# Attention of a hybrid decoder layer at three places of the order of work in place of seven

## The reference

```
h = rmsnorm(x, g_mix);  proj = h @ w_in            # columns: q, k, v (512 each), u (2 x 512), two gates (1024 each)
o = moba_attention(q, k, v)                         # 8 heads of 64; one block of 256, so plain causal attention
branch_a = o @ w_attn_up
z = u_a * sigmoid(u_g);  z = causal depthwise conv(z), 31 taps;  z = silu(layernorm(z))
branch_c = z @ w_conv_pw + b_conv_pw
x = x + (sigmoid(gate_a) * branch_a + sigmoid(gate_c) * branch_c) @ w_out
h = rmsnorm(x, g_ffn);  x = x + relu(h @ w_ff1)^2 @ w_ff2
return rmsnorm(x, g_final)
```

## Time and profile before

| | |
|---|---|
| median of 3 runs | 351.67 us |
| span of the profiled execution | 350.3 us |
| TensorE (PE) busy | 344.2 us, 98% |
| VectorE (DVE) busy | 251.5 us, 72% |
| ScalarE (ACT) busy | 192.1 us, 55% |
| chain of work that ended last | TensorE 98% of the span |

### The profile page before, as it was taken

One profiled execution on the slowest core, in us unless ns is written; L12 is line 12 of the kernel. 1 busy time (PEld: TensorE's weight loads), 2 busy tenths in 40 slices (PEclk: granted clock), 3 DMA queues, 4 the chain that ended last, 5 costly groups with the idle time before them and its releaser, 6 DMA issues.

```text
span 350.3 us, 4670 instructions
## 1 busy us (share of the span) xinstructions
PE 344.2 (98%) x1766; PEld 289.5 (83%) x1766; DVE 251.5 (72%) x313; ACT 192.1 (55%) x236; POOL 3.5 (1%) x13
## 2 busy tenths in 40 slices
PE   8999999999999999999999999999999999999994
PEld 5889988787778888888888888888888888889884
DVE  2969999899999889965666946639466394563813
ACT  4985644698796358434674535515355163551534
POOL 1000000000000000000000000000000000000000
PEclk9999999999999999999999999999999999999998
DMA  8999455534353365783647472944729537260003
GB/s 278 349 387 377 155 206 156 206 122 153 121 198 130 120 239 156 265 254 110 198 157 227 152 252 90 299 180 128 248 102 301 178 121 243 115 239 0 0 0 120
DMA packets 34429, 64.23 MB, mean 183 GB/s; under 512 B 1360, under 2 KB 6000, under 8 KB 34416
## 3 DMA queue, kind: packets, MB, share of 16 engines
q1 hardware_dynamic: 34056, 63.56, 54.0%
q10 hardware_dynamic: 360, 0.49, 0.4%
HBM read 63.00 MB, written 1.05 MB: 183 GB/s over the span
## 4 chain that ended last, share of the span: by engine, by line
PE 98%; DVE 0%; issue 0%; DVEq 0%; ACT 0%
PE ps L971 20%; PE ps L972 19%; PE ps L973 19%; PE ps L1230 17%; PE ps L1238 9%; PE ps L958 4%; PE ps L1018 2%; PE ps L1122 1%; PE ps L1121 1%; PE ps L1123 1%; PE ps L1029 1%; PE ps L1072 1%; PE ps L1097 1%; PE ps L998 1%; PE ps L1191 0%; PE ps L1282 0%
## 5 line engine op out<-in xcount | busy, mean ns | idle before, releaser
L971 PE MATMUL ps<-w_hi,a_lo 128*128 128x512 f32 x256 | 100.9, 394 | 0.0
L972 PE MATMUL ps<-w_hi,a_hi 128*128 128x512 f32 x256 | 99.8, 390 | 0.0
L973 PE MATMUL ps<-w_lo,a_hi 128*128 128x512 f32 x256 | 99.7, 390 | 0.0
L899 DVE TENSOR_TENSOR w_lo<-raw,w_hi 128x2048 fp32r<-128x2048 f32 x28 | 63.5, 2287 | 6.2 <-ACT w_hi L623 6.2
L405 ACT CAST w_hi<-raw 128x2048 fp32r<-128x2048 f32 (+1 forms) x30 | 53.7, 1799 | 19.9 <-PE ps L973 19.7
L1230 PE MATMUL ps<-b_both,w_hi 128*128 128x512 f32 x256 | 61.3, 390 | 0.0
L674 DVE TENSOR_TENSOR w_lo<-raw,w_hi 128x2048 fp32r<-128x2048 f32 x26 | 59.3, 2285 | 1.7 <-ACT w_hi L405 1.7
L623 ACT CAST w_hi<-raw 128x2048 fp32r<-128x2048 f32 x28 | 52.8, 1914 | 7.5 <-PE ps L973 7.5
L971 PEld LDWEIGHTS ps<-w_hi,a_lo 128*128 128x128 f32 x256 | 48.1, 188 | 10.1 <-issue 0.5
L973 PEld LDWEIGHTS ps<-w_lo,a_hi 128*128 128x128 f32 x256 | 48.0, 188 | 10.2
L972 PEld LDWEIGHTS ps<-w_hi,a_hi 128*128 128x128 f32 x256 | 48.1, 188 | 9.4
(11 more groups left out here) (138 smaller groups left out, 302.5 us busy)
## 6 DMA issues: line engine op xcount, KB each, us to landing
raw<-in_w_ff_dram SPq DMA_DIRECT2D x32, 1024.0 KB, 5.4
raw<-in_w_in_dram SPq DMA_DIRECT2D x14, 1024.0 KB, 5.9
raw<-in_w_out_dram SPq DMA_DIRECT2D x4, 1024.0 KB, 5.3
raw<-in_w_in_dram SPq DMA_DIRECT2D x14, 256.0 KB, 5.7
raw<-in_w_attn_up_dram SPq DMA_DIRECT2D x2, 1024.0 KB, 5.2
raw<-in_w_conv_pw_dram SPq DMA_DIRECT2D x2, 1024.0 KB, 5.1
res<-in_x_dram SPq DMA_DIRECT2D x2, 512.0 KB, 3.9
raw<-in_w_in_dram SPq DMA_DIRECT2D x4, 128.0 KB, 4.1
```

Source lines behind the costliest of these rows:

```text
L899: nc.vector.tensor_tensor(w_lo[:, slot], raw[:, slot], w_hi[:, slot].bitcast(F32), ALU.subtract).then_inc(lo_made, 1)
L971: nc.tensor.matmul(dst, lo[:, tok], w_hi[:, slot, k], start=start, stop=False, skip_group_check=seeded)
L972: nc.tensor.matmul(dst, hi[:, tok], w_hi[:, slot, k], start=False, stop=False, skip_group_check=seeded)
L973: return nc.tensor.matmul(dst, hi[:, tok], w_lo[:, slot, k], start=False, stop=stop, skip_group_check=seeded)
```

## The change

Scores, transposes and values are each done for two pairs at a time. The second pair of a group gets buffers of its own: banks `(4, 5)` and `(6, 7)` by `pair_banks(p)` for scores and later for the transposed blocks, and two parts of `nat` that are free then for probabilities and their transposed copy. Scores of pairs 0 and 1 stand behind unit 9, of 2 and 3 behind unit 12. Transposes of a group of two stand inside units 12 and 15, after the first tile of tokens, and its values behind the same unit. Outputs of pairs 0 and 1 go to bank 2, emptied by one copy of both, and block 5 is taken from that bank before (now in `take`'s usual place); unit 14, which writes bank 2, waits for that copy. The transposes of the convolution move from behind unit 16 into unit 17.

On ScalarE the converts around the scores move: the one of iteration 10 (unit 13) to iteration 9, ahead of the exponentials, the one of iteration 13 (unit 16) likewise to 12; at 12 and 15 the convert stands behind the copies of the probabilities. On VectorE the maxima of two pairs stand at the top of iterations 9 and 12, both inverses with three convolution steps between them behind the split; the convolution steps are dealt out anew; the layer norm goes with `S_LN` from iteration 16 to 17.

```diff
-S_ATT = 9
+S_SCORES = {9: (0, 1), 12: (2, 3)}
+S_VALUES = (12, 15)
+S_O_OUT = 14
+CONV_BETWEEN = 3
-S_OLO = S_ATT + 6
-S_GATE = 14
-S_LN = 16
+S_OLO = 15
+S_GATE = 16
+S_LN = 17
-CONV_AT = {..., 8: 6, 9: 5, 10: 8, 11: 11, 12: 12, 13: 11, 14: 10, 15: 5}
+CONV_AT = {..., 8: 6, 9: 6, 10: 6, 11: 6, 12: 15, 13: 12, 14: 11, 15: 6}
...
+        probs_of = (probs[:], nat[:, 0, 0:768])
+        probs_t_of = (probs_t[:], nat[:, 1, 0:768])
+        def pair_banks(p):
+            return (TB, SB0)[p % 2]
+        def o_pair(p):
+            if p < 2:
+                return ps[:, 2, p * T:p * T + T]
+            return ps[:, pair_banks(p) + 1, T:2 * T]
...
 # ScalarE, iteration n
-                if n and n + AHEAD < U_LOOP + AHEAD_LOOP and n not in GLU_AT:
+                if n and n + AHEAD < U_LOOP + AHEAD_LOOP and n not in GLU_AT and n not in S_VALUES and n - 1 not in S_SCORES:
                     high(n + AHEAD)
+                if n in S_VALUES:
+                    group = S_VALUES.index(n)
+                    probs_out(2 * group)
+                    probs_out(2 * group + 1)
+                    high(n + AHEAD)
+                    o_out(group)
+                if n in S_SCORES:
+                    high(n + AHEAD + 1)
+                    for p in S_SCORES[n]:
+                        exps(p)
+                    for p in S_SCORES[n]:
+                        normalise(p)
...
 # VectorE, iteration n (row_max, then the layer norm at S_LN, then low(n + 3), then:)
+                if n in S_SCORES:
+                    first, second = S_SCORES[n]
+                    inverse(first)
+                    conv_products(n, slice(0, CONV_BETWEEN))
+                    inverse(second)
                 if n != S_OLO:
-                    conv_products(n)
+                    conv_products(n, slice(CONV_BETWEEN if n in S_SCORES else 0, None))
...
 # TensorE, unit n
+                if n == S_O_OUT:
+                    pe.wait_ge(ot_made, 1)
                     unit(n, ...,
                          (lambda: glu_transposed(GLU_AT[n])) if n in GLU_AT else
+                         (lambda: pairs_transposed(S_VALUES.index(n))) if n in S_VALUES else
+                         conv_transposed if n == S_LN else None)
+                if n == S_VALUES[0]:
+                    pe.wait_ge(evac, GA)
+                if n in S_VALUES:
+                    group = S_VALUES.index(n)
+                    values(2 * group)
+                    values(2 * group + 1).then_inc(pv_done, 1)
+                if n in S_SCORES:
+                    for p in S_SCORES[n]:
+                        scores(p)
```

More of the change, by code:

```diff
@@ L60 @@
 CONV += [(tap, c) for tap in range(10, TAPS) for c in range(4)]
-CONV_AT = {2: 6, 3: 12, 4: 9, 5: 9, 6: 9, 7: 7, 8: 6, 9: 5, 10: 8, 11: 11, 12: 12, 13: 11, 14: 10, 15: 5}
+CONV_AT = {2: 6, 3: 12, 4: 9, 5: 9, 6: 9, 7: 7, 8: 6, 9: 6, 10: 6, 11: 6, 12: 15, 13: 12, 14: 11, 15: 6}
 assert len(CONV) == sum(CONV_AT.values()) == (TAPS - 1) * 4
@@ L195, in tile_chunks, with o_group @@
             return ps[:, bank + t, :].rearrange("p (c t) -> p c t", c=4)
-        def o_pair():
-            return ps[:, TB + 1, T:2 * T]
+        def pair_banks(p):
[4 more added lines that the diff above has]
+            return ps[:, pair_banks(p) + 1, T:2 * T]
+        def o_group(group):
+            if group == 0:
+                return ps[:, 2].rearrange("p (c t) -> p c t", c=2)
+            return ps[:, TB + 1:SB0 + 2:2, T:2 * T]
         def chunks(bank):
@@ L475, in exps @@
                 act.wait_ge(nbias_made, p + 1)
+                bank, rows = pair_banks(p), probs_of[p % 2]
                 for h in range(2):
-                    nc.scalar.activation(probs[:, 256 * h:256 * h + 256], ps[:, SB0 + h, 0:256], ACT.Exp,
+                    nc.scalar.activation(rows[:, 256 * h:256 * h + 256], ps[:, bank + h, 0:256], ACT.Exp,
                                          bias=nbias[:, p, h:h + 1], scale=q_scale[:, 1:2], accum_out=psums[:, p, h:h + 1])
                 for h in range(2):
-                    last = nc.scalar.activation(probs[:, 512 + 128 * h:640 + 128 * h], ps[:, SB0 + h, 256:384],
+                    last = nc.scalar.activation(rows[:, 512 + 128 * h:640 + 128 * h], ps[:, bank + h, 256:384],
                                                 ACT.Exp, bias=nbias[:, p, 2 + h:3 + h], scale=q_scale[:, 0:1],
@@ L489, in normalise, with o_out @@
                 for h in range(2):
-                    part = probs[:, 256 * h:256 * h + 256]
+                    part = probs_of[p % 2][:, 256 * h:256 * h + 256]
                     nc.scalar.activation(part, part, ACT.Copy, scale=rinv[:, p, h:h + 1])
                 for h in range(2):
-                    part = probs[:, 512 + 128 * h:640 + 128 * h]
+                    part = probs_of[p % 2][:, 512 + 128 * h:640 + 128 * h]
                     last = nc.scalar.activation(part, part, ACT.Copy, scale=rinv[:, p, 2 + h:3 + h])
                 last.then_inc(norm_made, 1)
-            def o_out(p):
-                act.wait_ge(pv_done, p + 1)
-                nc.scalar.copy(o_t[:, p], o_pair()).then_inc(ot_made, 1)
+            def o_out(group):
+                act.wait_ge(pv_done, group + 1)
+                nc.scalar.copy(o_t[:, 2 * group:2 * group + 2], o_group(group)).then_inc(ot_made, 1)
             def probs_out(p):
                 act.wait_ge(p_tr, p + 1)
-                if p:
-                    act.wait_ge(pv_done, p)
-                nc.scalar.copy(probs_t[:], ps[:, TB:TB + 2, :].rearrange("p b n -> p (b n)")[:, 0:768]).then_inc(pt_made, 1)
+                if p > 1:
+                    act.wait_ge(pv_done, 1)
+                bank = pair_banks(p)
+                nc.scalar.copy(probs_t_of[p % 2], ps[:, bank:bank + 2, :].rearrange("p b n -> p (b n)")[:, 0:768]).then_inc(pt_made, 1)
             def set_bias(col):
@@ L546, in _ @@
                     queries_out()
-                elif n < U_ATTN and n % 2 == 1 and 0 < n // 2 < GA:
+                elif n < U_ATTN and n % 2 == 1 and 0 < n // 2 <= GA:
                     take(n // 2)
[L549 to L557, removed]
+                if n in S_VALUES:
[10 more added lines that the diff above has]
+                        normalise(p)
                 if n < U_ATTN and n % 2 == 1 and n // 2 > GA:
@@ L564, in _ @@
                 if n == S_OLO:
-                    act.wait_ge(ot_made, PAIRS)
+                    act.wait_ge(ot_made, 2)
                     nc.scalar.copy(b_hi[:, 0:CC], o_t[:]).then_inc(o_hi, 1)
@@ L719, in _, with conv_products @@
             low_pair(3, 1, lo_made)
-            def conv_products(step):
-                for m in conv_share(step):
+            def conv_products(step, part=slice(None)):
+                for m in conv_share(step)[part]:
                     tap, c = CONV[m]
@@ L736, in row_max @@
                 dve.wait_ge(mask_made, 1)
-                diagonals = ps[:, SB0:SB0 + 2, P:3 * P]
+                bank = pair_banks(p)
+                diagonals = ps[:, bank:bank + 2, P:3 * P]
                 nc.vector.tensor_tensor(diagonals, diagonals, mask[:].rearrange("p (h s) k -> p h (s k)", h=1).to_broadcast([P, 2, 2 * P]),
@@ L740, in row_max @@
                 dve.wait_ge(masked, p + 1)
-                nc.vector.tensor_reduce(smax[:, p, 0:2], ps[:, SB0:SB0 + 2, 0:256], AX.X,
+                nc.vector.tensor_reduce(smax[:, p, 0:2], ps[:, bank:bank + 2, 0:256], AX.X,
                                         ALU.max).then_inc(max_made, 1)
-                nc.vector.tensor_reduce(smax[:, p, 2:4], ps[:, SB0:SB0 + 2, 256:384], AX.X,
+                nc.vector.tensor_reduce(smax[:, p, 2:4], ps[:, bank:bank + 2, 256:384], AX.X,
                                         ALU.max).then_inc(max_made, 1)
@@ L775, in _ @@
                                                 ALU.mult).then_inc(q_scaled, 1)
-                if n == S_ATT:
+                if n in S_SCORES:
                     dve.wait_ge(q_scaled, 3)
-                if S_ATT <= n < S_ATT + PAIRS:
-                    row_max(n - S_ATT)
+                    for p in S_SCORES[n]:
+                        row_max(p)
                 if n == S_LN:
@@ L864, in _ @@
                     low(n + AHEAD)
-                if S_ATT <= n < S_ATT + PAIRS:
-                    inverse(n - S_ATT)
+                if n in S_SCORES:
[3 more added lines that the diff above has]
+                    inverse(second)
                 if n != S_OLO:
-                    conv_products(n)
+                    conv_products(n, slice(CONV_BETWEEN if n in S_SCORES else 0, None))
                 if n == S_OLO:
@@ L1067, in scores @@
             def scores(p):
+                if p > 1:
+                    pe.wait_ge(pt_made, p - 1)
                 for s, at, keys in ((1, 0, 256), (0, 256, 128)):
@@ L1071, in scores @@
                         rows = slice(HD * h, HD * h + HD)
```

(24 more changed lines are left out.)

6 lines of the change are left out of this document (removed).

## The result

The changed kernel takes 355.21 us (median of 4 runs, 354.84 to 355.96) against 351.53 of the kernel before on the same chip: ratio 1.0104, 95% interval 1.0092 to 1.0116, 3.7 us slower. Forecast were 353.4 us and a range of 352.0 to 356.4: the right side and inside the range, but half of the loss was missing from the forecast.

A forecast was written before the change was run, and what follows sets the result against it. TensorE's own work was taken to bound the kernel. Fewer mode changes (-1.44 us) and a new wait for the normalised rows (+3.2) gave +1.8, added to the median of 351.67: 353.4 us, range 352.0 to 356.4.

The forecast's parts named there:

- The gain of 1.44 us: TensorE, attention between units 9 and 15: 7 changes of the array's mode instead of 15, 8 x 0.18 us saved.
- Joins of one kind: TensorE, groups of one kind side by side: pay nothing between them; full changes at all four joins would take 0.72 us.
- a change of mode: TensorE, switching between full, score and value products: 0.18 us each.
- No cost on ScalarE: Moved converts and later exponentials on ScalarE stay covered by TensorE's units, so they cost nothing.
- The idle time at the third mask: VectorE at the second place reaches the mask at 85.1, scores allow it at 87.8: 2.7 us idle.
- the second inverse: VectorE at the first place waits for the second pair's exponentials: 0.5 us idle.
- The wait itself: TensorE in unit 18 wants the normalised rows at 122.3, VectorE has them at 125.5: 3.2 us.
- Main sum: Whole kernel: gain of 1.44 us against a wait of 3.2 us, +1.8 us.
- rival (a): The wait in unit 18 lowers the granted clock, adding 2.9 us: 356.3 us; chance 0.18.
- The main case: Whole kernel: gain and wait without a fall of the clock, 353.4 us, bounded at 352.4 to 354.2; chance 0.68.
- the engine worked at the lower level of 1.2 GHz: TensorE at the kernel's start: 16 transposes took 3.2 us, 0.2 each against 0.11, read as the lower clock.
- I see no second wait behind: TensorE after the normalised rows in unit 18: no further wait, and nothing that wins the time back.

The follow-up runs named there:

- e10: Changed kernel with nine convolution steps moved from iteration 12 to 11, one from 9 to 8, and a fourth step between the inverses: 350.14 us.
- e2: Changed kernel with seven convolution steps moved from iteration 12 to 11, layer norm still behind the split: 350.82 us.
- e1: Changed kernel with VectorE's layer norm ahead of the split for unit 19 again: 353.32 us.
- e5: Kernel before with only VectorE's layer norm one iteration later, behind the split for unit 19: 351.75 us.
- e9: Changed kernel with seven convolution steps moved from iteration 12 to 11, one from 9 to 8, and a fourth between the inverses: 350.75 us.
- e4: Changed kernel with 12 products of zeros on TensorE ahead of its wait for the normalised rows: 353.65 us.
- e7: Changed kernel with four convolution steps moved from iteration 12 to 11: 351.70 us.

## Why the prediction was right, and where it was not

- **The gain of 1.44 us** was right: -1.43 in D of e10, where no wait is left, and -1.43 in medians (350.14 against 351.57). Joins of one kind cost nothing (the second pair of scores 0.65 against 0.64), a change of mode 0.175, as the mean of two, against 0.18.
- **No cost on ScalarE**: right; behind the start of the kernel no wait of TensorE in any trace is for the probabilities or a convert. Exponentials of the first pair started 4.5 us after the first scores, forecast was 4.6.
- **The idle time at the third mask**: 2.82 us, forecast 2.7; at the second inverse 0.27, forecast 0.5. It is one of three parts of the wait: without it the wait is 0.2 (e2), without the split ahead of the layer norm 0.7 (e1), and the late layer norm alone, without the idle time and the earlier TensorE, makes none (e5). e9 adds that filling idle time is not enough: what counts is how much of VectorE's work stands behind the third mask. The wait itself, counted as the time beyond a full stream, is 124.66 - 121.34 - 0.23 = 3.1 us, forecast 3.2.
- **Main sum**: +1.8 us for a full clock, and e4 gives 1.7 in D and 1.8 in medians (353.65 against 351.86).
- **What failed is the weight of rival (a)**, "Chance 0.18", and its argument "Against it: it is fully busy right up to that wait and again after it". That is no protection: the clock fell all the same, in the trace after and, by their times and clocks (0.988 to 0.993 over the span, with 0.997 in the profile before), in all four runs. The likeliest case should have been main sum plus rival: 351.53 + 1.8 + 2.9 would be 356.2. The price of 2.9 us, from slow work that the forecast put at about 5.9 us without a sum for it, was met in the profiled run (6.0 us of slow work, 2.9 lost in C), which was also the slowest (355.96 us, clock 0.988); in the median of 355.21 it is about 1.9. The main case alone, bounded at 352.4 to 354.2, missed the measured time; the range of 352.0 to 356.4 held only because it took in a rival that I thought unlikely, and that is luck in part. Of the Trainium skill, TensorE: Matmul & The Clock Gate, section HAM oscillation, I had written that by its rule alone 356.3 would be the forecast. That left out the section's condition on the length of a gap, which the wait falls somewhat short of, as forecast (3.2 us) and as measured (2.9). That an idle stretch halves the clock and the work behind it starts slow is what this trace shows (0.50 over 124 to 130.6); that 2.9 us was enough goes beyond the section, and the measurement decides.
- That at the start "the engine worked at the lower level of 1.2 GHz" rests on the pace of the transposes alone (0.2 us against 0.11); the granted clock of the profile reads 1.00 there.
- "I see no second wait behind" held for the changed kernel, but for a reason that I had not seen: e1 shows that VectorE was nearly as late for unit 20, where the forecast had no margin worked out. In the changed kernel the first wait hid this, and it didn't take the slow stretch: e4 has the same delay at a full clock and no wait at unit 20 either.

## What to carry to other kernels

Count the changes of the array's mode (rows by columns of the products), not the places: each costs 0.18 us here, and transposes of full size, at 0.11 us each, paid no change wherever they stood in the stream. When work is grouped on the engine that bounds the time, look at the other engines' programs for an instruction that now waits for the group with independent work queued behind it; that work has to go ahead of it, and it helps only if it crosses that point. And price a wait of the array twice: here 1.4 us of wait cost 1.6 (D of e7 against e10), while 2.9 us of it cost 2.9 more through the clock in the profiled run and 1.9 more in the medians. Where the wait couldn't be removed, products of zeros in it gave that part back (e4).

## What the runs showed that was not expected

The clock fell in the middle of a span in which TensorE was otherwise never idle, behind a wait of 2.9 us (for 6.8 us, until 130.7) and, in four of six runs by their clocks, behind one of 2.2 (for 3.4 us in the trace), not behind 1.4, nor behind 0.7 and 1.6 that stood 9 us apart. Where between 1.4 and 2.2 us it begins to fall, and why the same kernel goes either way, no run here shows. The pace at the start varies as well: 16 transposes of the input took 3.2 us in the trace before and 2.1 in the one after, which shifts all that follows by 0.8 us. The first products of the two kernels are the same, so I take it for chance and not for the change.
